# Attention scores from split queries: the second pass on half of TensorE's rows, for two heads side by side

## The reference

```python
qb = q.reshape(bn, nb, BLOCK, N_KV_HEADS, GQA_GROUP, HEAD_DIM)      # 8 blocks, 2 kv heads, 4 queries each, 64
kk = jnp.concatenate([jnp.pad(kb, pad)[:, :nb], kb], axis=2)        # previous and own block of 128 keys
scores = jnp.einsum('bnqhgd,bnkhd->bnhgqk', qb, kk,
                    preferred_element_type=jnp.float32) * (HEAD_DIM ** -0.5)
scores = jnp.where(mask[None, :, None, None, :, :], scores, NEG_INF) # causal, window of 128
probs = jax.nn.softmax(jnp.concatenate([scores, sink], axis=-1), axis=-1)[..., :2 * BLOCK]
out = jnp.einsum('bnhgqk,bnkhd->bnqhgd', probs.astype(vv.dtype), vv)
```

## Time and profile before

| | |
|---|---|
| median of three runs | 949.66 us (949.49 to 949.93) |
| the profiled execution's own time | 949.13 us |
| its span in the profile | 947.3 us |
| TensorE (PE) busy | 938.1 us, 99% of the span, 4423 matmuls |
| weight loads (PEld) busy | 778.5 us, 82% |
| DVE busy | 657.3 us, 69% |
| ACT busy | 435.9 us, 46% |
| GpSimd (POOL) busy | 189.3 us, 20% |

### The profile page before, as it was taken

One profiled execution on the slowest core, in us unless ns is written; L12 is line 12 of the kernel. 1 busy time (PEld: TensorE's weight loads), 2 busy tenths in 40 slices (PEclk: granted clock), 3 DMA queues, 4 the chain that ended last, 5 costly groups with the idle time before them and its releaser, 6 DMA issues.

```text
span 947.3 us, 11501 instructions
## 1 busy us (share of the span) xinstructions
PE 938.1 (99%) x4423; PEld 778.5 (82%) x4423; DVE 657.3 (69%) x713; ACT 435.9 (46%) x651; POOL 189.3 (20%) x182
## 2 busy tenths in 40 slices
PE   8999999999999999999999999999999999999997
PEld 7988888888888888888888888888888888888886
DVE  6645797666655899777777787778776653535668
ACT  5525445544433555445444544344444454435353
POOL 3301000000111424242223243443431100000021
PEclk9999999999999999999999999999999999999999
DMA  6999971005322236386343446464647776677545
GB/s 225 271 343 213 210 145 46 23 23 178 134 89 90 89 107 205 133 190 177 123 133 100 145 118 131 107 143 111 138 90 208 212 235 210 220 267 259 186 154 200
DMA packets 114248, 151.16 MB, mean 160 GB/s; under 512 B 6289, under 2 KB 66193, under 8 KB 114193
## 3 DMA queue, kind: packets, MB, share of 16 engines
q1 hardware_dynamic: 100737, 118.63, 38.7%
q0 software_dynamic: 13456, 31.79, 16.8%
HBM read 113.17 MB, written 60.29 MB: 183 GB/s over the span
## 4 chain that ended last, share of the span: by engine, by line
PE 97%; DVE 1%; DMA 0%; ACT 0%; POOL 0%; issue 0%; DVEq 0%; POOLq 0%; SPq 0%; ACTq 0%
PE ps L1660 30%; PE ps L1661 30%; PE ps L1662 30%; PE ps L1670 1%; PE ps L1795 1%; PE ps L1818 1%; PE ps L1796 1%; PE ps L1804 1%; PE ps L1822 1%; DMA xin<-in_x 0%; DVE hlo L1168 0%; DVE ps L1185 0%; PE ps L1708 0%; DVE x2b L1471 0%; DVE x2b L1477 0%
## 5 line engine op out<-in xcount | busy, mean ns | idle before, releaser
L1660 PE MATMUL ps<-hhi,whi 128*128 128x512 f32 (+1 forms) x240 | 90.3, 376 | 0.5 <-DVE hlo L1168 0.5
L1662 PE MATMUL ps<-hhi,wlo 128*128 128x512 f32 (+1 forms) x240 | 88.5, 369 | 0.0
L1661 PE MATMUL ps<-hlo,whi 128*128 128x512 f32 (+1 forms) x240 | 88.5, 369 | 0.0
L699 POOL TENSOR_TENSOR w_sums<-wraw 128x1024 f32<-128x1024 f32 x20 | 48.4, 2421 | 185.7 <-DVE w2lo L1417 63.0
L661 POOL TENSOR_SCALAR meansq<-sumsq 128x1 f32<-128x1 f32 x28 | 9.9, 352 | 372.7 <-ACT yg L1072 170.8
L1031 ACT ACTIVATE yg<-ps,par_b 128x1024 f32<-128x1024 f32 x21 | 25.3, 1207 | 57.9 <-DVE ps L1543 57.9
L1662 PEld LDWEIGHTS ps<-hhi,wlo 128*128 128x128 f32 x240 | 45.2, 188 | 7.7
L1660 PEld LDWEIGHTS ps<-hhi,whi 128*128 128x128 f32 x240 | 45.3, 189 | 7.6 <-DVE hlo L1168 0.7
L1661 PEld LDWEIGHTS ps<-hlo,whi 128*128 128x128 f32 x240 | 45.3, 189 | 7.0
L1491 DVE SCALAR_TENSOR_TENSOR yg<-ps,par_a,yg 128x1023 f32<-128x1023 f32 x22 | 28.2, 1283 | 26.9 <-ACT yg L1031 26.9
L1660 PE MATMUL ps<-h2hi,whi 128*128 128x512 f32 x116 | 45.4, 391 | 0.2 <-DVE wraw L1178 0.2
(11 more groups left out here) (269 smaller groups left out, 2716.2 us busy)
## 6 DMA issues: line engine op xcount, KB each, us to landing
wraw<-in_ffn_w_up SPq DMA_DIRECT2D x42, 512.0 KB, 5.2
s_dram<-in_ffn_w_down POOLq DMA_DIRECT2D x6, 2816.0 KB, 27.9
wraw<-r_dram SPq DMA_DIRECT2D x44, 256.0 KB, 3.7
wraw<-s_dram SPq DMA_DIRECT2D x44, 256.0 KB, 4.8
r_dram<-cst SPq DMA_DIRECT2D x33, 256.0 KB, 2.8
wraw<-act_dram SPq DMA_DIRECT2D x33, 256.0 KB, 3.6
wraw<-in_ffn_w_down SPq DMA_DIRECT2D x33, 256.0 KB, 4.4
wraw<-in_w_in SPq DMA_DIRECT2D x14, 512.0 KB, 10.3
```

Source lines behind the costliest of these rows:

```text
L699: pool.tensor_tensor(w_sums[:, 0:2, :], raw[:, 0:4:3, :], raw[:, 2:3, :].broadcast_to([P, 2, HALF]), ALU.add)\
L1660: pe.matmul(acc, w_hi, x_hi, start=first, stop=False, skip_group_check=looped)
L1661: pe.matmul(acc, w_hi, x_lo, start=False, stop=False, skip_group_check=looped)
L1662: return pe.matmul(acc, w_lo, x_hi, start=False, stop=last, skip_group_check=looped)
```

## The change

The scores' pass with `k_lo` takes only the rounded queries as weights, that is 64 of the 128 partitions. For the head e = 1 the two parts trade places in `q_parts`: the rounded part goes to partitions 64 to 127 and the rest to 0 to 63. So the rounded part of head e lies in the rows `own_rows(e)`, and the `k_lo` matmul of e = 0 uses rows 0 to 63 of the array and that of e = 1 rows 64 to 127. The loops of `score` are turned inside out: g outside, e inside, and for g = 0 the two whole matmuls with `k_hi` come first, for g = 1 the two half-row matmuls with `k_lo` do. A unit thus issues two whole matmuls, four on half the rows (e = 0, 1, 0, 1), and two whole ones. Their number (eight) and the keys that they stream stay as they were. The product of q_lo and k_lo is no longer part of the sum.

```diff
@@ -393,6 +393,10 @@
+        def own_rows(e):
+
+            return slice(e * HD, (e + 1) * HD)
@@ -815,7 +819,7 @@
                 for e in range(2):
-                    act.activation(q_parts[0:HD, :, 2 * j + e, :],
+                    act.activation(q_parts[own_rows(e), :, 2 * j + e, :],
                                    src[e * HD:(e + 1) * HD, :]
                                    .rearrange("p (b c) -> p b c", b=NT), ACT.Copy)\
                        .then_inc(q_rounded, 1)
@@ -1234,10 +1238,10 @@
                     dve.wait_ge(q_rounded, 2 * j + e + 1)
-                    last = dve.tensor_tensor(q_parts[HD:P, :, 2 * j + e, :],
+                    last = dve.tensor_tensor(q_parts[own_rows(1 - e), :, 2 * j + e, :],
                                              src[e * HD:(e + 1) * HD, :]
                                              .rearrange("p (b c) -> p b c", b=NT),
-                                             q_parts[0:HD, :, 2 * j + e, :], ALU.subtract)
+                                             q_parts[own_rows(e), :, 2 * j + e, :], ALU.subtract)
                 last.then_inc(q_ready, 1)
@@ -1787,13 +1791,17 @@
                 keys = slice(first * P, (b + 1) * P)
-                for e in range(2):
-                    for g in range(2):
-                        at = g * 2 * P + (first - b + 1) * P
-                        acc = ps[:, 4 + e, at:(g + 1) * 2 * P]
-                        q = q_parts[:, b, 4 * kv + 2 * g + e, :]
-                        pe.matmul(acc, q, k_hi[:, kv, keys], start=True, stop=False)
-                        last = pe.matmul(acc, q, k_lo[:, kv, keys], start=False, stop=True)
+                for g in range(2):
+                    at = g * 2 * P + (first - b + 1) * P
+                    acc = [ps[:, 4 + e, at:(g + 1) * 2 * P] for e in range(2)]
+                    q = [q_parts[:, b, 4 * kv + 2 * g + e, :] for e in range(2)]
+                    for whole in ((True, False), (False, True))[g]:
+                        opens = whole == (g == 0)
+                        for e in range(2):
+                            rows = slice(0, P) if whole else own_rows(e)
+                            keys_by_head = (k_hi if whole else k_lo)[rows, kv, keys]
+                            last = pe.matmul(acc[e], q[e][rows], keys_by_head, start=opens,
+                                             stop=not opens)
                 last.then_inc(scored, 1)
```

## The result

The changed kernel takes 951.91 us (median of 11 runs, 951.71 to 952.2); the kernel before, run beside it, takes 949.58 us (949.38 to 949.93). The ratio is 1.0024, with a 95% interval of 1.0016 to 1.0031: slower by 2.3 us. The forecast was 952.3 us and slower.

A forecast was written before the change was run, and what follows sets the result against it. The prediction took TensorE, busy 99% of the span, as the bound. Entering and leaving the half-row form (6.4 us) less the pairs' saving (3.8) gave +2.6 us, 952.3 us, with a range from 945.7 to 955.0.

The forecast's parts named there:

- TensorE's stream sets the time: Attention stage: a microsecond more or less in TensorE's own stream moves the end by about a microsecond.
- The pairs save 3.8 us: Scores: half-row matmuls of both heads run side by side, four in two steps, saving 0.238 a unit (0.22 where b is 0).
- Entry 0.21, exit 0.19, 6.4 us in all: Scores: going into and out of the half-row form costs 0.40 us in each of 16 units.
- ACT's and DVE's edits cost nothing; nor does the order: `round_q` and `low_q` keep instruction count and shape, costed at nothing; the new matmul order only shifts `scored`.
- What the profile would show: Each unit: two pairs about 0.12 apart, PEld gaps of 0.3 to 0.4, about 0.2 each side, 1.11 us; no new wait.
- (a): Half-row matmuls of each unit: entry and exit cost nothing, pairs run together; -3.8 us, 945.9 us; chance 19%.
- (b): Half-row matmuls: the two halves' weight loads come one after the other, stalls stay; +5.9, 955.6 us; chance 12%.
- (c): Half-row matmuls: halves run one after another without stall, 949.7 us, or a cheap stall eats the gain, 949.1 us; chance 11%.

The follow-up runs named there:

- same_rows: Changed kernel with both heads' rounded queries in partitions 0 to 63, so all four half-row matmuls of a unit use the same array half: 955.47 us.
- both_ends: Changed kernel with half-row pairs at both ends of a unit, two blocks of one pair instead of one block of two: 956.02 us.
- lo_twice: Changed kernel with the half-row pass issued twice in each unit, eight half-row matmuls in one block: 955.58 us.
- beside_attend: Changed kernel with half-row matmuls only in odd slots 3 to 15, right behind the attended values; other nine units as in the kernel before: 949.24 us.
- heads_apart: Changed kernel with the four half-row matmuls of a unit issued head by head, e = 0 then e = 1: 951.85 us.

## Why the prediction was right

The direction, the mechanism and the size held: +2.6 forecast, +2.3 measured. By its steps:

- *TensorE's stream sets the time.* Held: leaving the pass out saved 7.25 of the 7.5 us that its matmuls take.
- *The pairs save 3.8 us.* Held, and 0.1 to 0.2 too much: taking them away cost 3.6 us. (The four "instructions" that the prediction counts in the attended values are four records, of two float32 matmuls: L1818 issues 32 and leaves 64. The earlier trace rows count records too, so the comparison holds.) That the column halves' behaviour carries over to the rows was an assumption then; the paired records and the run with both heads in the same rows show it.
- *Entry 0.21, exit 0.19, 6.4 us in all.* A little too much. Entry and exit were 0.19 each in the 14 units of 256 keys, and where b is 0 the two together cost only 0.07 + 0.22 = 0.29 a unit (0.91 against 0.84, plus the pairs' 0.22). 14 x 0.38 + 2 x 0.29 = 5.9 us; same_rows measured the same 5.9. This is the term that was mis-sized, by 0.5 us; the pairs' gain, overrated too, took part of that back, so the forecast came out 0.3 us too high. Of the 0.5, 0.2 comes from the b = 0 units, to which I had carried the full 0.40 over although had shown a cheaper exit there (0.15). Why these are cheaper was not tried.
- *ACT's and DVE's edits cost nothing; nor does the order.* Held: 949.62 against 949.57 us.
- *What the profile would show.* The two pairs were there, the unit took 1.10 for the 1.11 forecast, and no wait came up. Three marks were off. The pairs are 0.22 apart, not 0.12, as the first is recorded from the start of its load. The 0.2 on each side does not stand at one matmul but in halves at two, 0.09 before the first and 0.10 between it and the next. And there was no idle gap of 0.3 to 0.4 us at PEld before the block and behind it: behind the last load that ended at about 105.55 (0.19 from 105.36) the gap was 0.12, and from 105.97 to 106.11 it was 0.14. The gaps of the earlier trace rows were long because loads of the matmuls before them, which last 0.22 to 0.23, lie further apart. So such a gap seems to measure the step of the work before it more than the stall.

The rivals: (a), a change of form for nothing, is out by both_ends, which has the same matmuls and 25 more changes of form (9 x 2 + 7) and is 4.1 us slower, 0.16 each. (b), loads that don't pair, is out by the loads' records and by lo_twice, where four more half-row matmuls cost 0.23 and not 0.44. (c), halves that run one after another or a stall of 0.10 each way, is out by the pairs and by the 0.19 each way. The Trainium skill's rule in "TensorEngine Tiling (Array Packing)", Key Properties, that a change of mode drains TensorE, holds for rows as for columns here: 0.19 us each way. About half of that is the weight load that follows, since no load goes ahead across the change: the first half-row pair lasts 0.38 as recorded and the next 0.28. The offset between tiles of different row groups that "TensorE: Matmul & The Clock Gate", Part 3, gives (about 4 ns) fits pairs that start within the 10 ns that the rows resolve.

## What to carry to other kernels

In this kernel matmuls on half the rows (or half the columns) ran two at a time, but a block of them must save more than its entry and exit cost, here 0.38 us, so more than three steps of 0.119. Put many of them together, and put them where the form changes anyway: behind the half-column matmuls the entry added nothing, and only the exit of 0.19 stood against the 0.24 that two pairs save. Price such a change before it is made from any other change of form that the trace already holds, and look at each size separately.

## What the runs showed of the hardware that was not expected

- Half columns straight to half rows costs no more than half columns to whole. In slot 5 the first matmul of the scores starts 0.32 behind the last of the attended values in every case, whole in the kernel before and in the changed one, half-row in both_ends and in beside_attend; beside_attend gained 0.05 a unit by it.
- The pairing does not need neighbours in the order of issue: in heads_apart the second head's first matmul overtook the first head's second one.
- An exit into float32 transposes of 128 columns cost 0.15 us (0.59 against 0.44), one into matmuls of 256 columns 0.19. Which property of the transposes makes the difference was not tried; their loads are recorded as shorter (0.14 against 0.19), and the first transpose lasts 0.33 where the others last 0.27, which would fit a shorter load left uncovered.
